# Part of a row sum moved behind a weight subtraction, and a block selection moved from VectorE to GpSimd

## The reference

```python
k = l2norm(heads(kvq[..., :DN_WIDTH]))              # kvq: projections, short conv of 5 taps, silu
decay = jnp.exp(jnp.where(incl, gc[..., :, None] - gc[..., None, :], -jnp.inf))
lmat = jnp.where(strict, jnp.einsum('nbhid,nbhjd->nbhij', kb, kc) * decay, 0.0)
amat = lmat + jnp.eye(DN_CHUNK, dtype=lmat.dtype)   # 64 x 64 a chunk
sol = lax.linalg.triangular_solve(amat, rhs, left_side=True, lower=True, unit_diagonal=True)
v_new = u_i - jnp.einsum('bhck,bhkv->bhcv', w_i, s)          # one step of the scan over chunks
s_next = s * jnp.exp(gl_i)[..., None, None] + jnp.einsum('bhck,bhcv->bhkv', kd_i, v_new)
```

```python
m = jax.nn.silu(cond) @ w[:, :n * D_MODEL] + b[:n * D_MODEL]
```

## Time and profile before

| what | value |
|---|---|
| time of three executions | 2048.9, 2049.14, 2053.12 us, median 2049.14 us |
| time of the profiled execution | 2052.08 us |
| span of its core in the profile | 2050.2 us |
| TensorE busy | 1972.0 us, 96% |
| VectorE busy | 1521.6 us, 74% |
| ScalarE busy | 949.4 us, 46% |
| GpSimd busy | 1028.4 us, 50% |
| one head in the middle of the loop | 57.6 us |

### The profile page before, as it was taken

One profiled execution on the slowest core, in us unless ns is written; L12 is line 12 of the kernel. 1 busy time (PEld: TensorE's weight loads), 2 busy tenths in 40 slices (PEclk: granted clock), 3 DMA queues, 4 the chain that ended last, 5 costly groups with the idle time before them and its releaser, 6 DMA issues.

```text
span 2050.2 us, 36021 instructions
## 1 busy us (share of the span) xinstructions
PE 1972.0 (96%) x12502; PEld 1752.6 (85%) x12502; DVE 1521.6 (74%) x3446; ACT 949.4 (46%) x1695; POOL 1028.4 (50%) x641
## 2 busy tenths in 40 slices
PE   5799999999999998999999999999999999999997
PEld 2678888888888877889999999999998888888886
DVE  4788888888521137779889677777458888888888
ACT  3545554454342334334333478888533333333332
POOL 0345555554444475446899776666763322222222
PEclk8999999999999999999999999999999999999999
DMA  6323232223223354334788789999999999999993
GB/s 269 120 78 109 99 105 94 97 78 104 63 93 99 117 187 157 107 108 155 268 280 278 246 292 366 361 356 365 399 367 368 373 383 341 359 343 356 363 346 121
DMA packets 151777, 469.93 MB, mean 229 GB/s; under 512 B 15632, under 2 KB 46576, under 8 KB 148464
## 3 DMA queue, kind: packets, MB, share of 16 engines
q1 hardware_dynamic: 108064, 300.13, 41.9%
q0 software_dynamic: 36864, 134.23, 18.0%
q10 hardware_dynamic: 6736, 34.08, 4.1%
HBM read 415.38 MB, written 53.00 MB: 228 GB/s over the span
## 4 chain that ended last, share of the span: by engine, by line
PE 80%; DVE 11%; POOL 3%; DMA 2%; issue 1%; ACT 1%; SPq 1%; POOLq 0%; ACTq 0%; DVEq 0%
PE bank L2967 25%; PE bank L607 12%; PE bank L608 12%; PE bank L609 12%; PE bank L2954 4%; POOL w_lo L1288 2%; DVE dY L1620 2%; DVE cv L1603 2%; PE pair L607 1%; PE pair L609 1%; PE pair L608 1%; DMA rows<-peer_u,e_row 1%; PE bank L2556 1%; PE bank L2566 1%; PE bank L2899 1%
## 5 line engine op out<-in xcount | busy, mean ns | idle before, releaser
L1288 POOL TENSOR_TENSOR w_lo<-raw,w_hi 128x1024 fp32r<-128x1024 f32 x148 | 363.5, 2459 | 365.3 <-ACT w_hi L1025 162.7
L607 PE MATMUL bank<-lat_hi,w_hi 128*128 128x384 f32 (+2 forms) x1488 | 535.2, 360 | 4.2 <-DVE lat_lo L2069 2.6
L609 PE MATMUL bank<-lat_hi,w_lo 128*128 128x384 f32 (+2 forms) x1488 | 521.0, 350 | 0.0
L608 PE MATMUL bank<-lat_lo,w_hi 128*128 128x384 f32 (+2 forms) x1488 | 520.5, 350 | 0.0
L1427 POOL DMA_INDIRECT rows<-peer_v,e_row x128 | 135.4, 1058 | 338.8 <-DVE pair L2287 318.9
L607 PEld LDWEIGHTS bank<-lat_hi,w_hi 128*128 128x128 f32 x1488 | 280.7, 189 | 18.5 <-issue 4.8
L609 PEld LDWEIGHTS bank<-lat_hi,w_lo 128*128 128x128 f32 x1488 | 280.0, 188 | 17.8
L608 PEld LDWEIGHTS bank<-lat_lo,w_hi 128*128 128x128 f32 x1488 | 280.7, 189 | 13.4 <-issue 0.2
L1288 POOL TENSOR_TENSOR w_lo<-raw_more,w_hi 128x1024 fp32r<-128x1024 f32 x80 | 199.9, 2503 | 92.9 <-ACT w_hi L1025 64.0
L2967 PE MATMUL bank<-w_lo,c_hi 128*128 128x512 f32 x768 | 237.1, 389 | 0.0
L2967 PE MATMUL bank<-w_hi,c_lo 128*128 128x512 f32 x768 | 237.1, 389 | 0.0
(11 more groups left out here) (403 smaller groups left out, 3595.7 us busy)
## 6 DMA issues: line engine op xcount, KB each, us to landing
raw<-w SPq DMA_DIRECT2D x210, 512.0 KB, 4.3
raw_more<-w SPq DMA_DIRECT2D x142, 512.0 KB, 4.9
g_dram<-gs ACTq DMA_DIRECT2D x24, 1024.0 KB, 9.0
gu_dram<-gu SPq DMA_DIRECT2D x120, 192.0 KB, 5.7
gq<-g_dram SPq DMA_DIRECT2D x45, 512.0 KB, 9.0
gl<-gu_dram SPq DMA_DIRECT2D x28, 768.0 KB, 7.8
ada<-w_ada SPq DMA_DIRECT2D x32, 512.0 KB, 3.3
dY<-gc_dram SPq DMA_DIRECT2D x8, 768.0 KB, 4.2
```

What stands on the lines that cost most here:

```text
L607: nc.tensor.matmul(out, hi, rh, start=start, stop=False)
L608: nc.tensor.matmul(out, hi, rl, start=False, stop=False)
L609: return nc.tensor.matmul(out, lo, rh, start=False, stop=stop)
L1288: nc.gpsimd.tensor_sub(w_lo[:, slot, :], raw_at(slot % 2 if src is None else src), w_hi[:, slot, :].bitcast(F32)).then_inc(split_done, 1)
```

## The change

Four edits. First, of the four parts of the row sum, heads 0 to 6 add two where they added four, and the other two behind the first low part of `next_weights`, ahead of `lengths`; the last head keeps all four in place. Second, the two multiplications into `T` leave VectorE's `pack_blocks` and are done by GpSimd in a new function `block_entries`, behind `lengths`. Third, VectorE's `pack_blocks` moves within step 4 of the scan from behind `new_values` to between the second and third tap; `modulation` moves from step 3 to step 4, in front of the taps. Fourth, TensorE's `sum_columns` moves from the last slot of step 3 to the middle slot of step 4.

```diff
@@ -1305,10 +1305,24 @@
                 pool.wait_ge(vev, n * NCH)
                 nc.gpsimd.tensor_tensor(invr[:, :], rk[:, :], phalf[:, 0:NCH], ALU.pow).then_inc(invr_done, 1)
 
-            def next_weights(n):
+            def block_entries(n):
+
+                pool.wait_ge(lt, (n + 1) * (NG + NCH))
+                pool.wait_ge(invr_done, n + 1)
+                for z in range(2):
+                    if z:
+                        pool.wait_ge(sub_done, n * N_SUB + 1)
+                    nc.gpsimd.tensor_mul(T[half(z), :, :], Lt[half(z), :, half(z)],
+                                         rep(cst[half(z), C_NEAR:C_NEAR + HB], NCH)).then_inc(sub_done, 1)
+                pool.wait_ge(sub_done, n * N_SUB + 2)
+
+            def next_weights(n, more=None):
 
                 lo(0, n * 4 + 5)
+                if more is not None:
+                    add_modulation(more, range(2, 4))
                 lengths(n)
+                block_entries(n)
                 for j in range(1, 3):
                     lo(j, n * 4 + (5 + j))
 
@@ -1368,12 +1382,12 @@
 
             next_weights(0)
             inverse(0, False)
-            add_modulation(0, range(4))
-            next_weights(1)
+            add_modulation(0, range(2))
+            next_weights(1, 0)
             with pool.Fori(1, H - 1) as h:
                 inverse(h, True)
-                add_modulation(h, range(4))
-                next_weights(h + 1)
+                add_modulation(h, range(2))
+                next_weights(h + 1, h)
             inverse(H - 1, True)
             add_modulation(H - 1, range(4))
             for j in range(2):
@@ -1681,10 +1695,6 @@
 
             def pack_blocks(n):
 
-                dve.wait_ge(lt, (n + 1) * (NG + NCH))
-                for z in range(2):
-                    nc.vector.tensor_tensor(T[half(z), :, :], Lt[half(z), :, half(z)],
-                                            rep(cst[half(z), C_NEAR:C_NEAR + HB], NCH), ALU.mult).then_inc(sub_done, 1)
                 dve.wait_ge(sub_done, n * N_SUB + 2)
                 nc.vector.tensor_reduce(packed[:, 0:NCH * BLK].rearrange("p (c r) -> p c r", r=BLK),
                                         T[:, :, :].rearrange("p c (q r) -> p c r q", r=BLK), AX.X, ALU.add
@@ -1872,8 +1882,6 @@
                             tap(1)
                         if s == 2 and fin:
                             scale_output(h - 1)
-                        if s == 4:
-                            pack_blocks(n)
                         if s == 5:
                             substitute(n, range(3, BLK - 1))
                             gate_output(h)
@@ -1900,11 +1908,14 @@
                         if s == 2:
                             decay_sums(n)
                         if s == 3:
-                            modulation(h, bank[1])
                             key_norms(n)
                         if s == 4:
-                            for i in range(4):
-                                tap(i)
+                            modulation(h, bank[1])
+                            tap(0)
+                            tap(1)
+                            pack_blocks(n)
+                            tap(2)
+                            tap(3)
 
             def whole_conv(o):
 
@@ -2649,7 +2660,7 @@
 
                     if (s, slot) == (0, 0):
                         pe.wait_ge(att_done, h * 4 + 4)
-                    if (s, slot) == (3, 2):
+                    if (s, slot) == (4, 1):
                         if fin:
                             pe.wait_ge(out_done, h * 2)
                         pe.wait_ge(ada_acc, (h + 1) * (KB - 1))
```

## The result

| | kernel before | changed kernel |
|---|---|---|
| median, lowest and highest of 4 executions each | 2050.30, 2048.90 to 2053.12 us | 2038.15, 2035.58 to 2039.87 us |
| the profiled execution, and its span | 2052.08, 2050.2 us | 2037.75, 2035.9 us |
| one head in the middle of the loop, mean of six | 57.54 us | 56.01 us |

The ratio is 0.9937, with a 95% interval of 0.9921 to 0.9952: 12 us faster, with 2038.5 us forecast. The changed kernel ran again later, beside other executions of the kernel before: 2040.06 against 2051.81 us.

What follows compares the result with a forecast made beforehand. TensorE was taken to bound the kernel, waiting for VectorE's held decays in steps 1 and 2. Terms -15.1 - 0.7 + 6.0 - 0.9 = -10.7 us gave 2038.5 us from 2049.14, range 2033 to 2045.

Steps and rivals of the forecast that it cites:

- Part 1: Steps 1 and 2: without additions beside the decays, TensorE's waits for `Vn` and `Rd` go, -15.1 us; state product, -0.7.
- rival B: Steps 1 and 2: exponents, casts or key products become late, a third to a half of 15.8 us lost; chance 0.12.
- Part 2: Step 4: the fourth moved addition holds `rk`, TensorE waits 0.86 us a head for `Rd`, +6.0 us over seven heads.
- rival A: Milder lock in the new place: only `kdr` held, -13.7 us, chance 0.18; or nothing held, -16.7 us, chance 0.08.
- Part 3: Products into `T`: VectorE sheds 1.12 us a head where TensorE is full, worth nothing; the reduction doesn't wait for GpSimd.
- Part 4: Head 0's bare blocks: products take 2.8 us on VectorE, 1.9 us on GpSimd ahead of the low part, -0.9 us.
- The sum: Whole kernel: -15.1 - 0.7 + 6.0 - 0.9 = -10.7 us, from median 2049.14 to 2038.5 us.
- Rival C: TensorE's `sum_columns`: the additions deliver `row` too late; slower from 2.6 us of slip on; chance 0.06.
- 4 us of slip: ScalarE's cast ahead of the low part 4 us later: 1.5 us a head lost, 10.2 in all, 2058 us.
- Rival D: Steps 1 and 2: waits stem from something else, such as a load, and stay; within 0.2% of before; chance 0.06.

Runs made afterwards that it cites:

- two-and-two order: Changed kernel with two of the four moved additions ahead of the first low part, right behind the decays, and two behind it: 2034.44 us, again 2033.24 us.
- block selection as before: Products on VectorE and reduction directly behind step 4's new values: 2042.49 us against the changed kernel, 2032.82 us against the two-and-two order.
- short additions: Kernel before with the four additions of the last two parts cut to 8 of 512 columns: 2033.94 us, ratio 0.9918.
- all four ahead of the low part: Changed kernel with all four moved additions right behind the twelfth decay, ahead of the first low part: 2068.45 us, ratio 1.0087.
- sums in their old place: Changed kernel with the sums of `row` back in step 3's last slot and `modulation` back in step 3: 2079.92 us, ratio 1.0137.

## Why the prediction was right

**Part 1, -15.1 and -0.7 us.** Right, and a little too small. From `cwm`, step 3's solve starts at 15.04 us in the changed kernel and at 17.38 to 17.80 us before: 2.3 to 2.8 us a head, 2.5 in the mean of six, where 15.8 us over seven are 2.26. The doubt about ScalarE (rival B, half of it) came to nothing.

**Part 2, +6.0 us.** Right in mechanism and size for six of the seven heads: `rk` is held, not only `kdr`, and 0.83 us are lost a head where 0.86 were said; with 0.67 in the first head it is 5.7 us in seven. `rk` takes 1.08 us, about 1.1 forecast. Some luck is in it. The forecast had `rk` only 0.18 us behind the start of the fourth addition, it is 0.25 us, and in the first head, where it comes 0.01 us ahead of that start, rival A is what happened: `rk` slips in and `kdr` alone is held. Where `rk` comes behind the start of the addition, rival A is wrong for its six elements, and right for single ones. That there were 5.6 us to save with another place, the two-and-two order confirms.

**Part 3, nothing in the loop.** Right for the change as made, shown by the block selection as before (55.09 and 56.01 us). The reason given was too broad. "TensorE is full in steps 3 to 5" is no licence to add 1.12 us to VectorE anywhere in them: between the taps they cost 0.4 us. The kernel before had them in a gap. Two products and their hand-over take 2.08 us on GpSimd where 1.9 were said, and the reduction waits for none of it.

**Part 4, -0.9 us.** Right in kind, and 0.3 us too large. The printed waits differ by 6.67 - 5.81 = 0.86 us, but over the kernels here they are 4.8 to 7.9 us, by what TensorE does ahead of them. Counted from TensorE's matmul on `vT`, which waits for the coupling matrices, to the one behind the blocks, it is 11.06 to 11.18 us in the six kernels with the products on VectorE, and 10.36 to 10.53 us in the eight profiles with the products on GpSimd: some 0.6 us.

**The sum.** -10.7 us forecast, -12.2 and -11.8 us between the medians. The lengths of the heads give 1.53 a head where 1.40 were said (15.8 - 6.0 over seven); that is 0.9 us, and the rest of the difference is within the interval. That the time itself, 2038.15 us, lies 0.35 us from the 2038.5 forecast is luck: the forecast started from a median of 2049.14 us, the kernel before has 2050.30 over four executions, 1.2 us more, and the gain was 1.5 us larger than forecast; the two nearly cancel.

**Rival C** did not happen to the change, but built as an own kernel it is real, and its working was a term short: behind a wait of 4 us TensorE lost another 2.6 us a head at the lower clock. The price given for 4 us of slip, 2058 us, has no such term. The rows showed only heads at a granted clock of 1.00, so the forecast didn't suffer.

**Rival D** fell with the short additions.

## What to carry to other kernels

List, for each long GpSimd instruction, what VectorE runs beside it, and put the GpSimd work beside instructions that read PSUM; a place is good only when the instructions on both sides of the slot, a few us each way, are known to be of that kind. Before work is taken off an engine, look whether it fills a gap that the engine has anyway: then it brings nothing, and its neighbours' order matters more than its time. When a change makes TensorE wait some us in one piece, price the wait and then the granted clock of the stretch behind it.

## What the runs showed of the hardware

**What a GpSimd instruction holds.** Beside additions of 1.3 us, in the changed kernel: a `tensor_scalar` of 6 elements that comes behind the addition's start is held (1.08 us against 0.17), and so is a copy of 3 elements, 0.90 us beside a pair of additions from 340.98 to 343.62, against 0.16 with no addition near (all four ahead of the low part, head 0). Single elements are not held (0.46 us for six). The Trainium skill, VectorE: DVE Perf Modes, "Mode 2×_2P — use both read ports for one tensor", lets `tensor_scalar` and copies use both read ports where the outermost dimension above one is even, or odd and equal on both sides; the three rows agree with that, and the short duration of an instruction protects nothing.

```profile
342.75 0.90 DVE L1627 COPY cwm<-cw 128x3 f32<-128x3 f32 x1
```

**What it does not hold.** A reciprocal of 6 elements, one input, takes 0.19 us at 141.11 in the changed kernel, inside the addition from 140.91 to 142.21. And `kdr`, two inputs in SBUF, takes 0.17 us at 366.06 inside the root `invr`, which runs from 365.96 to 367.30 and reads two tiles of 6 elements; it is the same in all eight heads of the kernel before. The Trainium skill, SBUF — State Buffer, "Who interferes with whom", has the shared ports taken for the whole of such an instruction. The additions and subtractions agree and this row doesn't: the root takes 1.33 us for 6 elements and 1.02 for 4 (`rno`), so most of it is hardly reading; no run here shows what part of it could hold, and the spans of GpSimd's records are rough.

**One slips between two.** Beside four additions and a low part in a row, VectorE's three decay sums take 0.33, 1.44 and 2.56 us from start to start (4.32 in all, the last 2.56): one is let in as each GpSimd instruction ends, and the next is held for the whole of the one that follows. It is so in all seven heads.

**The clock falls behind a wait of 3.4 us, but not each time.** Of seven heads with this wait (all four ahead of the low part) two kept 1.00, three fell to between 0.77 and 0.80 and two to 0.59 over the same 7.5 us. Behind 3.97 to 4.17 us (the sums in their old place) all seven fell, to between 0.50 and 0.71 over 5.8 us. The two levels are 2.4 and 1.2 GHz; in the first of these kernels matmuls of 256 columns follow each other at 0.21 us at the lower (374.05 to 375.33 us) and 0.12 at the higher (from 379.45 us).
